# A three-pass channel mixer with both projections in seven products

## The reference

```python
        pn = _rmsnorm(xp, ln_mlp[l])
        xp = xp + jnp.square(jax.nn.relu(pn @ w_up[l])) @ w_down[l]
...
    y_prompt = _rmsnorm(xp, ln_final)[:, N_META:]
```

## Time and profile before

| | us |
|---|---|
| median of 3 runs | 2339.76 (2338.31 to 2340.43) |
| the profiled execution | 2339.3 |
| its span | 2337.5 |
| mean granted PE clock | 0.996 of full |

### The profile page before, as it was taken

How to read it: one execution, slowest core, us unless ns; L and a number is a source line. 1 busy time by engine, 2 the same in 40 slices (tenths; PEclk the granted TensorE clock), 3 DMA queues, 4 the chain that set the end, 5 groups by cost and what they waited for, 6 DMA issues and landing times.

```text
span 2337.5 us, 37069 instructions
## 1 busy us (share of the span) xinstructions
PE 2306.4 (99%) x15645; PEld 2082.8 (89%) x15645; DVE 1219.4 (52%) x2074; ACT 810.4 (35%) x1443; POOL 534.7 (23%) x408
## 2 busy tenths in 40 slices
PE   8999999999999999999999999999999999999998
PEld 6788788878877877888999999999999999999998
DVE  6866665454454455423876676546443443444224
ACT  5445434333233223223434434523232232232321
POOL 3100001233342343322100000002332423323221
PEclk9999999999999999999999999999999999999999
DMA  9999435221221221222332222521211212212112
GB/s 371 327 248 221 145 99 207 98 66 65 87 81 63 81 91 55 74 102 65 111 123 82 92 63 84 180 91 38 89 64 64 85 57 76 77 58 74 46 46 85
DMA packets 86566, 247.33 MB, mean 106 GB/s; under 512 B 14465, under 2 KB 29953, under 8 KB 86401
## 3 DMA queue, kind: packets, MB, share of 16 engines
q1 hardware_dynamic: 54576, 162.94, 20.4%
q0 software_dynamic: 28800, 72.36, 11.2%
q10 hardware_dynamic: 3024, 9.67, 1.1%
...
## 4 chain that ended last, share of the span: by engine, by line
PE 95%; DMA 1%; DVE 1%; ACT 1%; SPq 1%; issue 0%; POOL 0%; DVEq 0%; ACTq 0%
PE bank L772 23%; PE bank L774 23%; PE bank L773 23%; PE aux L1039 5%; PE aux L1041 5%; PE aux L1040 5%; PE bank L1039 1%; PE bank L1041 1%; PE bank L1040 1%; PE aux L966 1%; PE aux L874 1%; DMA kept_lo<-w_lo 1%; PE aux L937 1%; PE aux L907 1%; PE aux L936 1%; DVE hb L2060 0%
## 5 line engine op out<-in xcount | busy, mean ns | idle before, releaser
L772 PE MATMUL bank<-a_hi,w_hi 128*128 128x358 f32 (+3 forms) x1600 | 579.3, 362 | 9.4 <-DVE w_lo L1906 6.5
L774 PE MATMUL bank<-a_hi,w_lo 128*128 128x358 f32 (+3 forms) x1600 | 563.5, 352 | 0.0
L773 PE MATMUL bank<-a_lo,w_hi 128*128 128x358 f32 (+3 forms) x1600 | 562.7, 352 | 0.0
L772 PE MATMUL bank<-b_hi,w_hi 128*128 128x358 f32 (+4 forms) x1280 | 450.8, 352 | 3.5 <-POOL w_lo L699 3.5
L773 PE MATMUL bank<-b_lo,w_hi 128*128 128x358 f32 (+4 forms) x1280 | 451.2, 352 | 0.0
L774 PE MATMUL bank<-b_hi,w_lo 128*128 128x358 f32 (+4 forms) x1280 | 451.0, 352 | 0.0
L699 POOL TENSOR_TENSOR w_lo<-w_st,w_hi 128x1024 fp32r<-128x1024 f32 x86 | 209.2, 2433 | 806.9 <-ACT w_hi L1141 806.9
L1141 ACT ACTIVATE w_hi<-w_st 128x1024 fp32r<-128x1024 f32 x208 | 219.3, 1054 | 419.1 <-PE aux L1041 250.3
L772 PEld LDWEIGHTS bank<-a_hi,w_hi 128*128 128x128 f32 x1600 | 301.0, 188 | 40.5 <-DVE w_lo L1906 8.5
L704 POOL TENSOR_TENSOR w_lo<-w_st,w_hi 128x512 fp32r<-128x512 f32 x192 | 248.3, 1315 | 366.0 <-ACT w_hi L1141 366.0
L773 PEld LDWEIGHTS bank<-a_lo,w_hi 128*128 128x128 f32 x1600 | 301.4, 188 | 27.0 <-issue 1.7
...
## 6 DMA issues: line engine op xcount, KB each, us to landing
...
```

The costliest lines, as they stand in the source:

```text
L772: pe.matmul(ps, wh, xh, start=(j == 0), stop=False)
L773: pe.matmul(ps, wh, xl, start=False, stop=False)
L774: mm = pe.matmul(ps, wl, xh, start=False, stop=(j == 7))
```

## The change

The channel mixer runs in three passes `q` over 328, 352 and 360 columns by two tiles (`MW`). Pass 0 follows the output projection of half 0 and takes 656 of its 1,008 columns; the 352 left over (`LEFT`) go with the first 352 of half 1 into pass 1; pass 2 has the last 720. The rest of x lies in DRAM between (`x1_d`, `bn_d`), with its loads and stores on ACT's queue. The output projection of half 0 has three tiles (`OUT_TILES`) instead of two, and the order of its last units changes (`OUT_UNITS`).

**Both projections in seven products.** Hidden units are in 8 groups of 512, none dense. Up: for each of two hidden blocks `j` seven products over four input blocks, 14 products of 12 matmuls. Down: four pairs, 28 products of 6 matmuls. The order of the seven is `ORDER`; `up_product` and `down_product` show what each waits for. In the first group of pass 0 and 1 the two hidden blocks go side by side (`UP_SEQ`).

**Operands of up.** The norm can't be applied behind the products any more. Before the first group of a pass, DVE norms the four quadrants (`n11`, `n12`, `n22`, `n21`), makes `t3`, `t2`, `t1`, `t6` and all low parts (`RIGHT_D`: each name has four steps, one for an input block), ACT the high parts (`RIGHT_A`); `first_group` and `rest_of_right` set their place. In pass 2 the operands of the first products are made in the down stage of pass 1's last group; there are 20 such DVE steps.

**Hidden blocks.** DVE gathers the products' sums in `tmp` (`sZ`, `sY`, `sV`), then `quarters`; `c12` and `c21` read a bank. ACT's order in a group is `up_stage` with `next_half` between. The takes of the first products of pair 0 stand inside `quarters(j=1)`. `to_basis` (before the first take of a pass) and the unmixing (`unmixed`, in the last group) change x to the basis of the seven states and back.

**Weights in halves.** A half is 128x512, in a ring of four places of the same `w_st`, `w_hi`, `w_lo`: 28 halves a group, 224 a pass, loaded by SP, rounded by ACT (`round_half`), subtracted by POOL (`split_half`). Sums of weights of all 8 groups, up and down, are made by DMA on POOL's queue in the first token mixer, one `sum_steps` behind every second weight block: 8 copies, 4 and 2 and 2 accumulating transfers a group.

**Around it.** The eight `add_input_square` of half 1 are on POOL, behind `reload(1)`, which waits for the last down product of pass 0. ACT has all eight `input_square` ahead of `round_x(1, 0)`, then the 16 squares of pass 0's final norm. The piece `RS` (row sums of half 1's input norm) is at slot 5 instead of 1. The final norm of pass 1 runs inside pass 2; at the end 16 tiles are scaled.

The core of the diff (of the operations, orders and waits that are named above; addresses and stores are left out):

```diff
+MW = [328, 352, 360]
+LEFT = META + 2 * MW[0]
+TILES = [[(0, 512), (512, 512)], [(0, MW[1]), (MW[1], MW[2]), (MW[1] + MW[2], MW[2])]]
...
+OUT_TILES = [[(META, MW[0]), (META + MW[0], MW[0]), (LEFT, MW[1])], TILES[1]]
...
+ORDER = [1, 5, 7, 6, 2, 3, 4]
...
+UP_SEQ = [[(i, j) for j in range(2) for i in ORDER],
+          [(i, j) for i in ORDER[:4] for j in range(2)] + [(i, j) for j in range(2) for i in ORDER[4:]]]
+FRONT_A, MID_A = ["s"], ["r22", "q22", "hi5"]
+BACK_A = ["r11", "hi0", "q11", "hi3", "hi2", "r21", "hi4", "q21", "hi1", "hi6"]
+FRONT_D, MID_D = ["sZ", "sY", "sV"], ["lo5"]
+BACK_D = ["lo0", "c12", "r12", "t3", "t2", "c21", "lo3", "lo2", "t1", "lo1", "lo4", "t6", "lo6"]
...
+RIGHT_D = []
+for _q in range(PASSES):
+    _n = lambda *names: list(names) if _q == 0 else [n for n in names if n[0] != "n" or (_q == 1 and n[-1] == "2")]
+    _steps = [(n, kb) for n in _n("n11") + ["lo0"] for kb in range(4)]
+    if _q:
+        _steps += [(n, kb) for n in _n("n12") + ["t3", "lo3"] for kb in range(4)]
+    else:
+        _steps += _chain(["n12", "t3"], "lo3", lag=1)
+    _steps += _chain(_n("n22") + ["t2"], "lo2", lag=1)
+    _steps += _chain(["lo5", "t1"], "lo1", lag=1)
+    _steps += [(n, kb) for n in _n("n21") + ["lo4"] for kb in range(4)]
+    _steps += _chain(["t6"], "lo6", lag=1)
+    RIGHT_D.append(_steps)
+RIGHT_A = [(n, kb) for n in ("hi0", "hi3", "hi2", "hi5", "hi1", "hi4", "hi6") for kb in range(4)]
...
-RS_SLOTS = [{4: 0, 9: 1}, {1: 0}]
+RS_SLOTS = [{4: 0, 9: 1}, {5: 0}]
...
+            def split_half(h):
+
+                pool.wait_ge(w_split, MLP0 + h + 1)
+                pool.tensor_tensor(w_place(w_lo, h), w_place(w_st, h), w_place(w_hi, h).bitcast(F32),
+                                   ALU.subtract).then_inc(w_ready, 1)
...
+            def sum_copies(g):
+
+                b0, e = blocks_of(g)
+                top, low = flat(wall[b0 + e:b0 + e + 2]), flat(wall[b0 + e + 2:b0 + e + 4])
+                dtop = flat(wall[b0 + KB:b0 + KB + PAIRS])[:, P * e:P * e + 2 * QW]
+                dlow = flat(wall[b0 + KB + PAIRS:b0 + 2 * KB])[:, P * e:P * e + 2 * QW]
+                for sums, w, a1, a2 in ((up_sums, HW, top, low), (down_sums, QW, dtop, dlow)):
+                    pool.dma_start(flat(sums[g, 0]), a2[:, 0:w]).then_inc(summed[g], 16)
+                    pool.dma_start(flat(sums[g, 2]), a1[:, 0:w]).then_inc(summed[g], 16)
+                    pool.dma_start(flat(sums[g, 1]), a1[:, 0:w]).then_inc(summed[g], 16)
+                    pool.dma_start(flat(sums[g, 3]), a1[:, w:2 * w]).then_inc(summed[g], 16)
...
+            def sum_steps(s, g0, g1):
+
+                for back, make in enumerate((sum_copies, sum_low, sum_three, sum_four)):
+                    if g0 <= s - back < g1:
+                        make(s - back)
...
+            for s in range(EARLY_SUMS + 3):
+                pool.wait_ge(w_ready, 2 + 2 * s)
+                sum_steps(s, 0, EARLY_SUMS)
...
+                    reload(n, n % 2)
+                    for b in range(1, KB):
+                        add_input_square(b)
+                    continue
...
+                def up_product(q, g, k):
+
+                    i, j = UP_SEQ[abreast(q, g)][k]
+                    h = half_no(q, g, k)
+                    b = BANK[i]
+                    if i == 2:
+                        pe.wait_ge(h_act, act_no(q, g, j, "s"))
+                    elif i == 3:
+                        pe.wait_ge(h_dve, dve_no(q, g, j, "sY"))
+                    elif i == 4:
+                        pe.wait_ge(h_dve, dve_no(q, g, j, "sZ"))
+                    elif g or q == 2:
+                        last = {X: 2, Z: 4, Y: 3, V_: 6}[b]
+                        pe.wait_ge(product_read, take_no(q if g else 1, (g - 1) % GROUPS, j + 2, last))
+                    elif j == 0:
+                        evacuated(pe, out_no(q, KB - 1, 2) - 3 + b)
+                    else:
+                        a = AUX[(q, "N2", 0)]
+                        drained(pe, {X: a - 1, Z: a, Y: a + 1, V_: a + 2}[b])
+                    if q == 2 and g == 1 and j and i in (6, 7):
+                        pe.wait_ge(n_root, 1 if i == 6 else 2)
+                    half_split(h)
+                    ps = group_bank(q, j, b)[:, 0:MW[q]]
+                    for kb in range(4):
+                        if g == 0 and j == 0:
+                            pe.wait_ge(r_dve, rd_no(q, f"lo{RIGHT[i]}", kb))
+                        mm = three(ps, h, P * kb, *right(q, RIGHT[i], kb), kb == 0 and i in OPENS,
+                                   kb == 3 and i not in (1, 5, 7))
+                    mm.then_inc(product_done, 1)
+
...
+                def down_product(q, g, d):
+
+                    j, n = divmod(d, len(ORDER))
+                    i = ORDER[n]
+                    h = half_no(q, g, UPS + d // 2)
+                    b = BANK[i]
+                    if i in OPENS:
+                        if j >= 2:
+                            pe.wait_ge(product_read, take_no(q, g, j - 2, {X: 2, Z: 4, Y: 3, V_: 6}[b]))
+                        elif b == X:
+                            pe.wait_ge(h_act, act_no(q, g, j, "r11"))
+                        else:
+                            pe.wait_ge(h_dve, dve_no(q, g, j, {Z: "c21", Y: "c12", V_: "sV"}[b]))
+                    else:
+                        pe.wait_ge(product_read, take_no(q, g, j, {2: 1, 3: 7, 4: 5}[i]))
+                    half_split(h)
+                    ps = group_bank(q, j % 2, b)[:, 0:MW[q]]
...
+                def up_stage(q, g):
+
+                    special = abreast(q, g)
+                    for j in range(2):
+                        k0 = 7 * j
+                        if not special:
+                            front(q, g, j)
+                            for k in range(4):
+                                next_half(q, g, k0 + k)
+                        middle(q, g, j)
+                        first_quarter(q, g, j)
+                        at = (8 + 3 * j) if special else k0 + 4
+                        next_half(q, g, at)
+                        next_half(q, g, at + 1)
+                        differences(q, g, j)
+                        next_half(q, g, at + 2)
+                        last_quarter(q, g, j)
+                        if j:
+                            next_half(q, g, UPS)
+                        fourth(q, g, j)
+                        if q == 2 and g == 1 and j == 0:
+                            for t in range(2):
...
+                    if part == 0:
+                        for b in range(KB):
                             input_square(1, b)
-                    if p == 0 and (m, t) == (KB - 1, 0):
-                        act.wait_ge(unit_done, last_unit(0, (2 * KB - 1) * NT[0]) + 1)
+                        act.wait_ge(product_done, product_no(0, GROUPS - 1, PRODUCTS - 1))
                         round_x(1, 0)
...
+                def gather(q, g, j, i):
+
+                    s_ = tmp[:, j, 0:MW[q]]
+                    dve.wait_ge(product_done, up_no(q, g, i, j))
+                    if i == 5:
+                        squared(q, g, j, "s")
+                    else:
+                        own(q, g, j, {7: "sZ", 6: "sY"}[i])
+                    step(tt(s_, s_, group_bank(q, j, BANK[i])[:, 0:MW[q]], ALU.subtract))
+
+                def middle(q, g, j):
+
+                    squared(q, g, j, "hi5")
+                    step(low(q, B22, j, hb(q, 2), -1.0))
+
+                def quarters(q, g, j):
+
+                    w = MW[q]
+                    h11, h12, h22, h21 = (hb(q, i) for i in range(4))
+                    s_ = tmp[:, j, 0:w]
+                    squared(q, g, j, "q11")
+                    step(low(q, B11, j, h11))
+                    dve.wait_ge(product_done, up_no(q, g, 3, j))
+                    step(stt(h12, group_bank(q, j, Y)[:, 0:w], -1.0, s_, ALU.mult, ALU.subtract))
+                    own(q, g, j, "c12")
+                    step(stt(h12, h12, 0.0, h12, ALU.max, ALU.mult))
+                    own(q, g, j, "r12")
+                    step(tt(h11, h11, h12, ALU.subtract))
+                    step(tt(h12, h22, h12, ALU.subtract))
+                    dve.wait_ge(product_done, up_no(q, g, 4, j))
+                    step(tt(h21, group_bank(q, j, Z)[:, 0:w], s_, ALU.add))
+                    squared(q, g, j, "hi3")
+                    step(low(q, T1, j, h11))
+                    squared(q, g, j, "hi2")
+                    step(low(q, T3, j, h12))
+                    own(q, g, j, "lo3")
+                    step(stt(h22, h22, -1.0, h11, ALU.mult, ALU.subtract))
+                    if j:
+                        take(q, g, 0, 1)
+                    squared(q, g, j, "q21")
+                    squared(q, g, j, "hi1")
+                    step(low(q, T2, j, h22))
+                    step(low(q, B21, j, h21))
+                    if j:
+                        take(q, g, 0, 5)
+                        take(q, g, 0, 7)
```

(59 more changed lines are left out.)

1334 lines of the change are left out of this document (753 added, 581 removed).

## The result

| | before | after |
|---|---|---|
| median | 2339.85 us | 2540.93 us (2540.0 to 2541.78) |
| ratio, 95% interval | | 1.086 (1.084 to 1.088) |
| span of the profiled execution | 2337.5 | 2538.3 |
| mean granted PE clock | 0.996 | 0.956 |

The kernel became 8.6% slower. The forecast was 2382 (2298 to 2435): the direction held, the size did not; the loss is 201 us instead of 43.

The account below looks back on a forecast made before the run. PE's work was taken to set the end, DVE and POOL mattering where PE waits for them. 2339.3 -111.7 -12 -5 +78 +57 +6 +23 +5 +3 = 2382.6; forecast 2382 us, range 2298 to 2435.

Parts of the forecast that it names:

- rival 1: The lock between DVE and POOL hardly bites: steady groups 15 us, first groups 47, total 2309 us; chance 0.25.
- Product work: Channel mixers' matmuls in seven products save 113.4 us; three-tile first output projection adds 1.7; together -111.7 us.
- Rival 4: Weight loads floor the matmul pitch, so 328 columns run no faster than 358: 2417 us; chance 0.05.
- Before's own waits and the start: Old waits in the first channel mixer go, -12 us; fewer copies issued at once at the start, -5 (0 to -9).
- The lock: In 21 steady groups, POOL's subtraction and DVE's two-SBUF-input instructions exclude each other: 3.7 us each, +78 (15 to 115).
- rival 2: The lock saturates, both chains at their top: steady groups 115 us, total 2420 us; chance 0.15.
- First groups: First group of each pass: DVE prepares operands before products; 27, 22 and 8 us, together +57 (40 to 75).
- Last groups: Pass 1's last group carries 20 operand steps and 8 unmixing operations among its takes: +6 us (0 to 12).
- Pass 0 to mixer 1: PE waits 16 us for reloads, POOL's sums and x rounding; clock recovery 3, late RS slot 4: +23 (15 to 28).
- Weight sums: DMA copies and accumulates of weights in the first token mixer, mostly hidden: +3 us (0 to 25).
- Rival 3: Accumulates at 6.4 us/MB hold POOL past block 26, output projection starves 30 us: 2410 us; chance 0.08.
- End: After the last PE product, 16 scalings instead of 8: +5 us (3 to 7).

Follow-up runs that it names:

- pool_short: Against the after kernel, POOL subtracts only the first 64 of the 512 columns of each weight half: 2380.96 us.
- norm1_short: Against the after kernel, pass 1's final norm inside pass 2 squares, sums and inverts 16 columns instead of 352, scalings kept: 2536.01 us.
- fill_first_down: Against the after kernel, PE runs 50 products with overwritten results in the wait of each pass's first down product: 2535.86 us.

## Why the prediction was right or wrong

The direction was right and the cause that was named is the largest one, but the forecast of 2382 missed by some 158 us. Against its terms, in rounded numbers, the first groups have 66 of them, the 18 steady groups 32, the last groups and the second of pass 2 34, the sums of weights with the start 23, the way from pass 0 to mixer 1 8, the end 3; the saving, with before's own waits, was some 10 better. Two steps failed:

- The lock was priced too low. The forecast differs from rival 1, where the lock hardly bites, by 73 us (63 in the steady groups, 10 in the first ones). Taking most of the hold away gave back 160 us in pool_short, and 135 and 132 where POOL still worked on every column.
- The first groups and the sums of weights were priced too low even without the lock: pool_short is at 2381, where rival 1 has 2309. Its first groups still lose 28, 29 and 35 us (47 in all by rival 1), and the sums cost 26 instead of 3.

Term by term:

- *Product work*, -113.4 with pitches from two widths: right. The matmuls of the channel mixers, each at its pitch, add up to 115 us less. Rival 4 (a floor under narrow matmuls) is out.
- *Before's own waits and the start*: -12 where 20 went, and the wait of 6.5 us for weights at the start is gone.
- *The lock*: right in kind, and the steady groups came at the top of their range, 5.5 us each where I took 3.7: rival 2. I had reckoned each chain with two or three held steps. In the trace r12, t3 and t1 are held most of the time, by 0.5 to 0.9 us on average: ACT's order puts two halves ahead of the step that waits for t3 and one ahead of that for t1, so POOL begins just when DVE does. The sign that I had named did not show: the low parts were to take well over 0.50 us, and those of line 2452 (all but lo5) stayed at 0.50 and 0.53 by their medians; in the steady group shown above POOL stands idle beside most of them. pool_short took 94 us from the steady groups, 31 from the first ones, and 30 from the last groups and the second of pass 2, where I had nothing for it beside the steady 3.7.
- *First groups*: the step that failed most. Terms 27, 22 and 8, measured 37, 39 and 47. In pass 2 I counted only the operands' chain and gave the final norm of pass 1, which shares ACT and DVE with it, no price at all. Its waits are of order: 17.5 us went with the order alone. The second group of pass 2 lost 19 us, for which I had only the steady 3.7; norm1_short leaves waits of 3.7 and 2.2 us there (3.7 and 3.9 in after), and what part of them is the scalings (`middle_out`) was not tried.
- *Last groups*: +6 for pass 1 and nothing for pass 0, each beside the steady 3.7; measured 19 and 13, the steady 5.5 included.
- *Pass 0 to mixer 1*: right in place and cause; the wait was reckoned at 16 and was 18.7. Behind it come 12 us in the mixer, of which I had 7.
- *Weight sums*: mis-sized, +3 for some 26. The sum of transfer times (300 to 414 us against 375) was near the truth; taking the hopeful side of it was the error. Rival 3, at 0.08, is what happened, on top of rival 2, since these cases do not exclude each other. My range treated them as alternatives; together they give 2448.
- *End*: +5, measured 8.
- *Clock*: up to the last product PE was at the 1.2 GHz level for 208 us, in before for 10. In the sum were 3 us for it. What it costs is not settled. An estimate of the most it can be, from the trace: in the slow stretches 430 matmuls are followed by the next after 1.5 to 2.3 times their pitch, and what that is beyond the pitch adds up to 55 us, in before to 4. Part of that would have been waits at full clock, as behind the first wait of pass 0 in fill_first_down. So up to 50 of the 201 us, which stand among the groups' losses above, may be clock.
